# Prompt attention of a hybrid decoder: the unit behind the meta tokens computed with rounded value products

## The reference

```python
keys = jnp.concatenate([jnp.pad(kb[:, :-1], shift), kb], axis=2)
vals = jnp.concatenate([jnp.pad(vb[:, :-1], shift), vb], axis=2)
...
mask = (diff >= 0) & (diff < WINDOW) & (kpos[:, None, :] >= 0)
o = attend_with_sink(qb, keys, vals, mask[None, :, None, None], sinks)
```

```python
p = jnp.exp(s - m)
p = p / (jnp.sum(p, axis=-1, keepdims=True) + jnp.exp(sink - m))
return jnp.einsum('...kgqs,...skd->...qkgd', p.astype(v.dtype), v)
```

## Time and profile before

| | |
|---|---|
| times of three runs | 955.08, 955.59 and 1718.46 us; median 955.59 |
| profiled execution, own time | 955.14 us |
| its span, first to last instruction | 953.3 us |
| PE busy | 933.8 us |
| DVE, ACT, POOL busy | 576.7, 479.9, 323.3 us |
| mean granted PE clock | 0.999 of full speed |

### The profile page before, as it was taken

The page is one execution under the profiler, slowest core; times in us unless marked ns, Lnnn a source line. Parts: engine busy times, 40 slices in busy tenths (PEclk is TensorE's granted clock), DMA queues, the critical chain, the costliest instruction groups (busy, mean ns, idle before and its releaser), DMA issues.

```text
span 953.3 us, 18522 instructions
## 1 busy us (share of the span) xinstructions
PE 933.8 (98%) x7276; PEld 876.1 (92%) x7276; DVE 576.7 (60%) x1444; ACT 479.9 (50%) x947; POOL 323.3 (34%) x257
## 2 busy tenths in 40 slices
PE   9999999999999999999999999999999999999998
PEld 7998999999998999989998889998899988998787
DVE  4235522554235621466698589856898568986782
ACT  6335713464235613376437665346562565526852
POOL 2442244233341244225624242522344223442500
PEclk9999999999999999999999999999999999999999
DMA  7522232432234221211534815247143562327303
GB/s 213 182 75 68 72 106 73 123 121 89 70 93 153 89 89 52 89 24 45 150 94 119 226 47 167 90 138 220 49 144 91 159 199 78 125 84 218 104 12 106
DMA packets 144615, 105.92 MB, mean 111 GB/s; under 512 B 10754, under 2 KB 135860, under 8 KB 144464
## 3 DMA queue, kind: packets, MB, share of 16 engines
q1 hardware_dynamic: 134536, 100.19, 34.9%
q10 hardware_dynamic: 9992, 4.54, 1.9%
HBM read 91.99 MB, written 16.79 MB: 114 GB/s over the span
## 4 chain that ended last, share of the span: by engine, by line
PE 85%; DVE 9%; issue 2%; ACT 2%; DMA 1%; POOL 1%; SPq 0%; DVEq 0%; ACTq 0%; POOLq 0%
PE pp L1298 21%; PE pp L1300 21%; PE pp L1299 21%; PE pS L1408 2%; PE pO L1640 2%; PE pO L1636 2%; PE pT_ L1626 2%; DVE s_in L2355 1%; PE pO L1587 1%; PE pS L1559 1%; PE pO L1463 1%; PE pO L1462 1%; PE pp L1350 1%; PE pS L1597 1%; PE pT_ L1432 1%
## 5 line engine op out<-in xcount | busy, mean ns | idle before, releaser
L711 POOL TENSOR_TENSOR w_lo_buf<-w_raw_buf,w_hi_buf 128x512 fp32r<-128x512 f32 x214 | 279.1, 1336 | 470.2 <-ACT w_hi_buf L787 285.3
L1298 PE MATMUL pp<-h_hi,w_hi_buf 128*128 128x280 f32 (+2 forms) x1248 | 375.8, 301 | 1.6 <-issue 1.6
L1300 PE MATMUL pp<-h_hi,w_lo_buf 128*128 128x280 f32 (+2 forms) x1248 | 362.7, 291 | 0.0
L1299 PE MATMUL pp<-h_lo,w_hi_buf 128*128 128x280 f32 (+2 forms) x1248 | 362.1, 290 | 0.0
L1298 PEld LDWEIGHTS pp<-h_hi,w_hi_buf 128*128 128x128 f32 x1248 | 234.8, 188 | 10.0 <-issue 7.8
L1299 PEld LDWEIGHTS pp<-h_lo,w_hi_buf 128*128 128x128 f32 x1248 | 234.9, 188 | 4.2 <-issue 3.3
L1300 PEld LDWEIGHTS pp<-h_hi,w_lo_buf 128*128 128x128 f32 x1248 | 235.1, 188 | 0.0
L787 ACT ACTIVATE w_hi_buf<-w_raw_buf 128x2048 fp32r<-128x2048 f32 (+1 forms) x55 | 104.2, 1894 | 49.3 <-DMA w_raw_buf<-in_w_ssm_in 31.5
L1826 DVE TENSOR_TENSOR x<-x,pp 128x272 f32<-128x272 f32 (+2 forms) x120 | 53.0, 442 | 78.1 <-PE pp L1300 77.3
L1298 PE MATMUL pp<-og_hi,w_hi_buf 128*128 128x280 f32 (+2 forms) x256 | 75.1, 293 | 2.8 <-DVE x L1826 1.7
L1300 PE MATMUL pp<-og_hi,w_lo_buf 128*128 128x280 f32 (+2 forms) x256 | 74.4, 291 | 0.0
(11 more groups left out here) (372 smaller groups left out, 1644.5 us busy)
## 6 DMA issues: line engine op xcount, KB each, us to landing
w_raw_buf<-in_w_attn_in SPq DMA_DIRECT2D x16, 1024.0 KB, 5.3
w_raw_buf<-in_w_ssm_in SPq DMA_DIRECT2D x16, 1024.0 KB, 6.0
w_raw_buf<-in_w_attn_out SPq DMA_DIRECT2D x8, 1024.0 KB, 5.2
s_in<-in_state_ssm SPq DMA_DIRECT2D x32, 256.0 KB, 4.2
out<-s_in SPq DMA_DIRECT2D x32, 256.0 KB, 3.4
w_raw_buf<-in_w_ssm_out SPq DMA_DIRECT2D x8, 1024.0 KB, 6.6
seg<-a_scratch SPq DMA_DIRECT2D x12, 512.0 KB, 5.3
w_raw_buf<-in_w_attn_in SPq DMA_DIRECT2D x8, 512.0 KB, 6.3
```

The lines of the kernel that those rows point to most:

```text
L711: ins = pool.tensor_tensor(low_buf(n)[:, piece], raw[n % RAW_SLOTS][:, piece], high_buf(n)[:, piece].bitcast(F32), ALU.subtract)
L1298: pe.matmul(dst, hi[:, k, cols], a_hi[:, k, tk], start=(k == 0), stop=False)
L1299: pe.matmul(dst, hi[:, k, cols], a_lo[:, k, tk], start=False, stop=False)
L1300: mm = pe.matmul(dst, lo[:, k, cols], a_hi[:, k, tk], start=False, stop=(k == depth - 1))
```

## The change

The unit `c` = 1 goes the way of `c` = 2 to 4. Block 4 of `tok` is set to zero once on POOL, so that the rows behind the 16 meta rows are zeros; ACT waits for that before it writes the first stage's meta rows (`tok_zero`). `tok_hi` and `tok_lo` get a fifth block. `copy_pT` has one piece for `c` = 1, `low_pT` no longer skips it, and `values` issues six rounded products for it, with block 4 as the block ahead. The counts of `pt_low` go from three to four a stage.

```diff
-        tok_hi = at("tok_hi", [P, 4, P], F32R)
-        tok_lo = at("tok_lo", [P, 4, P], F32R)
+        tok_hi = at("tok_hi", [P, 5, P], F32R)
+        tok_lo = at("tok_lo", [P, 5, P], F32R)
...
+            pool.memset(tok[:, 4, :], 0.0).then_inc(tok_zero, 1)
...
-                elif c == 1:
-                    act.activation(pT[0:16, 0:512], fT[0:16, 0:512], ACT.Copy)
-                    act.activation(pT[:, 512:1024], fT[:, 512:1024], ACT.Copy).then_inc(pt_ready, 1)
                 else:
                     act.activation(pT_hi[:, 0:1024], fT[:, :], ACT.Copy).then_inc(pt_ready, 1)
...
-                act.activation(tok_hi[:, :, :], tok[:, 0:4, :], ACT.Copy).then_inc(tok_high, 1)
+                act.activation(tok_hi[:, :, :], tok[:, 0:5, :], ACT.Copy).then_inc(tok_high, 1)
...
+                else:
+                    act.wait_ge(tok_zero, 1)
                 act.activation(tok[:, 0:4, :].rearrange("p c d -> p (c d)"), fT[:, 0:512], ACT.Copy)
                 act.activation(tok[0:16, 4, :], fT[0:16, 512:640], ACT.Copy)
...
-                    if 3 * s + c > 2:
-                        pe.wait_ge(pt_low, 3 * s + max(c, 2) - 2)
+                    if 4 * s + c > 1:
+                        pe.wait_ge(pt_low, 4 * s + c - 1)
...
-                    if c == 1:
-                        pe.matmul(pO[:, 0, :], tok[0:16, 4, :], pT[0:16, 0:512], start=True, stop=False)
-                        mm = pe.matmul(pO[:, 0, :], tok[:, 0, :], pT[:, 512:1024], start=False, stop=True)
-                    else:
-                        pe.wait_ge(tok_low, s + 1)
-                        for n, (t, p) in enumerate(((tok_hi, pT_hi), (tok_lo, pT_hi), (tok_hi, pT_lo))):
-                            if n == 2:
-                                pe.wait_ge(pt_low, 3 * s + c - 1)
-                            pe.matmul(pO[:, 0, :], t[:, c - 2, :], p[:, 0:512], start=(n == 0), stop=False)
-                            mm = pe.matmul(pO[:, 0, :], t[:, c - 1, :], p[:, 512:1024], start=False, stop=(n == 2))
+                    pe.wait_ge(tok_low, s + 1)
+                    before = 4 if c == 1 else c - 2
+                    for n, (t, p) in enumerate(((tok_hi, pT_hi), (tok_lo, pT_hi), (tok_hi, pT_lo))):
+                        if n == 2:
+                            pe.wait_ge(pt_low, 4 * s + c)
+                        pe.matmul(pO[:, 0, :], t[:, before, :], p[:, 0:512], start=(n == 0), stop=False)
+                        mm = pe.matmul(pO[:, 0, :], t[:, c - 1, :], p[:, 512:1024], start=False, stop=(n == 2))
...
-                dve.tensor_tensor(tok_lo[:, :, :], tok[:, 0:4, :], tok_hi[:, :, :].bitcast(F32),
+                dve.tensor_tensor(tok_lo[:, :, :], tok[:, 0:5, :], tok_hi[:, :, :].bitcast(F32),
...
-                if ORDER[u] in (0, 1, 5):
+                if ORDER[u] in (0, 5):
                     return
```

More of the change, by code:

```diff
@@ L375, in build @@
         par_tr, par_ready, ones_ready = sem("par_tr"), sem("par_ready"), sem("ones_ready")
+        tok_zero = sem("tok_zero")
         tok_high, tok_low, pt_low = sem("tok_high"), sem("tok_low"), sem("pt_low")
```

## The result

The changed kernel's median was 951.16 us (950.51 to 951.54, six executions), that of the kernel before, beside it, 955.59 us (954.17 to 959.76, five executions, with a mean of 956.33; a sixth, disturbed, took 1718.46 us and is left out). The ratio is 0.9945 [0.9924, 0.9966], 0.55% less time. By the medians that is 4.4 us, by the means 5.3 us, and either is more than the 3.0 us forecast. The profiled execution took 950.51 us, with a span of 948.7 us. Ratios in this document stand with their 95% interval; they need not be the quotient of the medians beside them.

A forecast was written before the change was run, and what follows sets the result against it. PE was taken to bound the kernel, busy 933.8 of 953.3 us. Profiled 955.14 us less four gains of 0.75 us (3.0), other engines costed at nothing, plus 0.2 for a median gave 952.3 us, range 951.1 to 954.2.

The forecast's parts named there:

- PE's gain at the place: From gate projection to next unit's transposes, PE takes 5.61 instead of 6.36 us: 0.75 a unit, 3.0 over four.
- Padding its rows to 128 can't lengthen the product by itself: At the meta block's float32 product on PE: 16 rows and 128 rows both take 1.05 us.
- the neighbouring turn as a working copy: PE's next turn, `c` = 2 with six rounded products, shows what `c` = 1 becomes: 5.61 us against 6.36.
- What the other engines pay: DVE's added 1.225 us subtraction fits its 2.37 us idle time, 0.75 to spare; ACT and POOL pay nothing.
- the division: DVE's division of the next weights stays 0.54 us ahead of the PE transposes that need it.
- the meta unit's division: Behind the longer `tok_lo` on DVE, its lead over PE's transposes shrinks from 0.32 to 0.18 us, costed at nothing.
- POOL's half slab: POOL's split beside the new DVE subtraction: neither slows, as 2.54 us with a subtraction against 2.53 without showed.
- DVE's path: Rival: the subtraction delays DVE's eviction and division, costing at most 0.48 us a unit, 957.2 us; chance 0.04.
- given back: Rival: behind the four places PE waits for a transfer or weight slab, losing the 3 us, 955.3 us; chance 0.06.
- Fewer passes only: Rival: at the four places PE gains only two passes, 0.23 us each, 1.8 us in all, 953.5 us; chance 0.08.
- The sum: Whole kernel: profiled 955.14 less 3.0 gives 952.1; 0.2 more for a median gives 952.3 us; chance 0.80.
- the Mamba stages must have kept their lengths: Sign in the changed kernel's trace, besides everything standing 3 us earlier at the fourth stage's end.

The follow-up runs named there:

- two products more: Changed kernel with two more rounded products, low weights by low values, at each of the four places; 953.98 us, ratio 0.9993.
- half the rounding: Kernel before with only the unit's own block as three rounded products, meta block unrounded over 16 rows; 954.79 us, ratio 0.9999.
- the padded kernel: Kernel before with the meta block zero-padded to 128 rows, products still unrounded float32; 953.49 us, ratio 0.9993.
- the 16-row kernel: Changed kernel with the meta block's three rounded products over 16 rows instead of 128; 956.3 us, ratio 0.9994.

## Why the prediction was right in kind and short in size

- **PE's gain at the place: right, 0.72 us for 0.75.** Six products 0.23 us apart, no idle time at the fifth, 5.64 us for 5.61, four times 0.72 = 2.9 us for 3.0.
- **Where the gain comes from: read wrongly.** "Padding its rows to 128 can't lengthen the product by itself" was true and missed the point: equal durations of 1.05 us hid that both products paid for the change between 16 and 128 rows. Padding alone gives 0.39 us, rounding the padded products another 0.33, rounding only the own block 0.16, and rounding without padding loses 0.45. These parts don't add up in any order, since each depends on which rows stand beside it. The reason given for 0.75 us a unit, the neighbouring turn as a working copy, was sound, since that turn has no such change of rows. The PEld row with 0.76 us of idle time ahead of the load at 87.17 was in the trace of before.
- **What the other engines pay: right.** DVE had 0.80 us to spare for 0.75; the division ends at 87.11, 0.57 us ahead of the transposes, for 0.54; the meta unit's division keeps 0.19 us for 0.18. One subtraction more was free, two cost 1.14 us a unit. POOL's half slab takes 2.56 us beside the new subtraction, for 2.53: no contention that matters.
- **The rivals.** The subtraction didn't come onto DVE's path, and nothing was given back: at the fourth stage's end everything stood 2.9 us earlier for the four places and stayed so. "Fewer passes only" is refuted as a size, 0.72 us against 0.46, but half of its mechanism holds: what a float32 product took beyond 0.86 us wasn't its own and belonged to its neighbours. It didn't stay, because the padding took the change of rows away; from there the rounding gives 2 x 0.86 - 6 x 0.23 = 0.34 us, measured 0.33.
- **The sum: this is the step that failed.** It took 955.3 us for the kernel before, from two executions, put the scatter at 0.5 us, and subtracted the gain at the places alone, with no term for the clock; "the Mamba stages must have kept their lengths" was its condition. Between the two profiled executions they did, to 0.2 us behind the slab at 445 us, and both had a clock of 0.999. In other executions of the kernel before they don't: the second profile lost 1.9 us there. The kernel before has a median of 954.9 to 956.8 us by session, and its executions reach 962. Of 103 of its executions in the three sessions, the 38 with a mean granted clock of at least 0.999 have a median of 954.46 us, the other 65 one of 956.42. All 12 executions of the changed kernel are at 0.999 or above, with a median of 951.15 us. So at the same clock the difference is 3.3 us: 2.9 at the four places and 0.4 that no run assigns. The further 2.0 us go with the lower clock in most executions of the kernel before; that the clock alone makes them is not shown. How many executions it meets also changes by session: 9 of 41, 11 of 35 and 18 of 27 had 0.999 or above. In the third session the median of before, 954.89 us, is 3.3 us above the changed kernel with one subtraction more. The range, 951.1 to 954.2 us, just held the time of 951.16, but not the difference: it allowed at most 4.2 us from 955.3, and 4.4 by medians or 5.3 by means were measured.

What stays open is why the changed kernel kept its clock in all of its 12 executions. With one subtraction more, 4 of 5 executions had 0.999 or above; with 28 rounds or two products more 7 of 11; with half the rounding 1 of 11; with 18 rounds none of 12. That PE's idle stretches come first is shown by the traces; which of them the clock answers with a fall isn't predicted by their length (2.20 us in the padded kernel without a fall, 1.69 us in the 16-row kernel with one at 905 us).

## What to carry to other kernels

Look at the weight loads, not only at the products: where a load starts with its product instead of with the one before, a change of the row count stands in the path, and padding a short operand with zeros can be worth as much as the rounding it was meant to allow. (The meta unit's own product, L1452 over 16 rows, still shows it: its load and the next one start with their products, at 80.33 and 80.74 us in the kernel before. No run padded that one.) On an engine that has little slack, read the margin of each neighbour in order (eviction, division, next reader); here margins read from rows were good to 0.1 us. And for a change of a few tenths of a per cent take the baseline's scatter from many executions with their granted clocks: two that agree within 0.5 us said nothing of a spread of 7.

## What the runs showed of the hardware

- Rounded products of 512 columns that alternate between 16 and 128 rows take 0.43 us each; with 128 rows throughout 0.23. An unrounded one takes 0.86 us between products of 128 rows, 1.05 beside one of 16.
- PE worked at the lower clock level behind idle times of 1.28, 1.69, 2.20 and 2.77 us, but idle times of 1.64, 1.69 and 2.20 us in other executions were followed by none.
- Loads ran ahead of products in flight where the columns of the stationary operand alternate between 16 and 128 (transposes 0.11 us apart), and did not where its rows do.
- With two rounds of start-up products fewer (18 in place of 20) the median was 4 us longer, in another session. The profiled execution, 6.5 us longer than the changed kernel's median, was at half clock from 14 to 21 us and from 120 to 123.5 us, and had a stall of 2.77 us at 117 us.
